# Last output projection of a two-block model as a 2x2 block product with seven multiplications

## What is computed

```python
def second_block(x, norm_g, w_in, q_norm_g, k_norm_g, rel_bias, w_out):
    ...
        mixed = jnp.concatenate([merge_heads(ya) * jax.nn.silu(ga),
                                 merge_heads(yb) * jax.nn.silu(gb)], axis=-1)
        x = x + jnp.einsum('bse,ed->bsd', mixed, w_out[layer])
    return x
```

## Time and profile before

| | |
|---|---|
| median of 3 runs | 1912.47 us (1911.5 to 1912.92) |
| profiled execution, first to last instruction (span) | 1910.9 us |
| TensorE (PE) busy | 1903.4 us, 100% of the span |
| TensorE weight loads (PEld) | 1586.7 us, 83% |
| VectorE (DVE) busy | 1172.9 us, 61% |
| ScalarE (ACT) busy | 817.9 us, 43% |
| GpSimd (POOL) busy | 112.1 us, 6% |
| last projection, first matmul to last | 1733.4 to 1907.7 us |

### The profile page before, as it was taken

The page is one execution under the profiler, slowest core; times in us unless marked ns, Lnnn a source line. Parts: engine busy times, 40 slices in busy tenths (PEclk is TensorE's granted clock), DMA queues, the critical chain, the costliest instruction groups (busy, mean ns, idle before and its releaser), DMA issues.

```text
span 1910.9 us, 27480 instructions
## 1 busy us (share of the span) xinstructions
PE 1903.4 (100%) x9126; PEld 1586.7 (83%) x9126; DVE 1172.9 (61%) x2193; ACT 817.9 (43%) x1603; POOL 112.1 (6%) x172
## 2 busy tenths in 40 slices
PE   9999999999999999999999999999999999999999
PEld 7788888888888888888888888888888888888887
DVE  6565687778877775634556565656564646466333
ACT  5653444544445434423444343434343434344211
POOL 0100011001111010001000000000000000000010
PEclk9999999999999999999999999999999999999999
DMA  8722232223232223344332222222222222223341
GB/s 323 297 89 88 78 99 78 71 71 99 77 77 77 69 73 112 123 152 143 121 116 72 91 90 88 93 88 93 88 89 92 71 102 79 88 88 121 137 160 66
DMA packets 33817, 202.09 MB, mean 106 GB/s; under 512 B 4592, under 2 KB 4720, under 8 KB 13296
## 3 DMA queue, kind: packets, MB, share of 16 engines
q1 hardware_dynamic: 23904, 165.95, 24.2%
q0 software_dynamic: 9728, 35.49, 6.8%
q10 hardware_dynamic: 144, 0.10, 0.0%
HBM read 193.10 MB, written 8.42 MB: 105 GB/s over the span
## 4 chain that ended last, share of the span: by engine, by line
PE 95%; DVE 2%; DMA 1%; ACT 1%; issue 0%; SPq 0%; DVEq 0%; ACTq 0%
PE gemm L1480 82%; PE pb L1480 12%; PE pb L1483 2%; DMA raw<-in_w 1%; DVE w_lo L829 1%; DVE act_lo L838 0%; DMA scratch<-in_memT 0%; ACT w_hi L398 0%; DVE scratch L1039 0%; ACT act_lo L435 0%; DVE parts L849 0%; DVE scratch L937 0%; ACT scratch L406 0%; ACT scratch L407 0%; ACT scratch L405 0%
## 5 line engine op out<-in xcount | busy, mean ns | idle before, releaser
L1480 PE MATMUL gemm<-act_hi,w_hi 128*128 128x512 f32 x2304 | 921.0, 400 | 0.2 <-DVE act_lo L838 0.2
L1480 PE MATMUL gemm<-act_lo,w_hi 128*128 128x512 f32 x2320 | 902.8, 389 | 0.1
L1480 PE MATMUL gemm<-act_hi,w_lo 128*128 128x512 f32 x2304 | 899.8, 391 | 0.0
L398 ACT ACTIVATE w_hi<-raw 128x512 fp32r<-128x512 f32 x616 | 337.3, 619 | 406.7 <-PE gemm L1480 385.9
L1480 PEld LDWEIGHTS gemm<-act_hi,w_lo 128*128 128x128 f32 x2304 | 432.4, 188 | 93.3
L1480 PEld LDWEIGHTS gemm<-act_lo,w_hi 128*128 128x128 f32 x2320 | 436.7, 188 | 83.4 <-ACT w_hi L398 0.4
L1480 PEld LDWEIGHTS gemm<-act_hi,w_hi 128*128 128x128 f32 x2304 | 433.4, 188 | 82.2 <-issue 0.8
L829 DVE TENSOR_TENSOR w_lo<-raw,w_hi 128x512 fp32r<-128x512 f32 x624 | 400.1, 696 | 144.7 <-ACT w_hi L398 137.2
L1480 PEld LDWEIGHTS pb<-scratch 128*128 128x128 f32 x932 | 136.0, 192 | 26.3 <-DVE scratch L1200 5.9
L1480 PE MATMUL pb<-scratch 128*128 128x128 f32 (+3 forms) x932 | 141.4, 279 | 2.2 <-DVE scratch L844 1.7
L1348 DVE SCALAR_TENSOR_TENSOR scratch<-gemm,scratch 128x512 f32<-128x512 f32 x24 | 16.6, 692 | 150.1 <-PE gemm L1480 149.9
(11 more groups left out here) (296 smaller groups left out, 1614.8 us busy)
## 6 DMA issues: line engine op xcount, KB each, us to landing
raw<-in_w SPq DMA_DIRECT2D x154, 1024.0 KB, 4.8
scratch<-in_rows_in POOLq DMA_DIRECT2D x6, 1024.0 KB, 8.5
big<-in_xT POOLq DMA_DIRECT2D x4, 1024.0 KB, 11.4
scratch<-rows POOLq DMA_DIRECT2D x16, 256.0 KB, 6.5
scratch<-in_xT POOLq DMA_DIRECT2D x16, 256.0 KB, 2.9
x<-big POOLq DMA_DIRECT2D x16, 256.0 KB, 2.3
scratch<-x POOLq DMA_DIRECT2D x16, 256.0 KB, 4.0
outT<-scratch POOLq DMA_DIRECT2D x15, 256.0 KB, 3.8
```

What stands on the lines that cost most here:

```text
L398: A(w_hi[slot][:, c], raw[slot][:, c], ACT.Copy).then_inc(sem["hi"], 1)
L1480: return nc.tensor.matmul(out, a, b, start=start, stop=stop, skip_group_check=skip)
```

## The change

The 16 output tiles are made in 8 pairs (outputs 2g and 2g+1). Of the 16 k-tiles, twelve (0 to 5 and 8 to 13) are taken as a 2x2 block product: six k-tiles against six, two outputs, and the 512 tokens in two halves of 256. The block product is made with seven products (Strassen in Winograd's form) instead of eight, each of 6 k-tiles x 3 matmuls of 256 columns. The four k-tiles 6, 14, 7, 15 (`REST`) are multiplied in the usual way, 512 columns wide, once for each output (R1, R2). The order on PE in each pair is M1 M6 M5 M7 M2 M3 R1 M4 R2 (nine products, 150 matmuls: 126 of 256 columns and 24 of 512; before 96 of 512).

New work for this: on GpSimd four sums of weight blocks per pair (each 128x768), and once the sums of token blocks, 24 operations of 128x256, during heads 6 and 7; their split into parts (`t_split`, `t_low`: six of 128x768 on each of ScalarE and VectorE); per pair on VectorE four half-width and one full-width addition that combine the products, on ScalarE one copy of M1. Weight parts are made by product, 768 columns at a time (512 for R1 and R2), in five slots instead of two buffers. SyncE loads six pieces per pair (four of 384 KB, two of 256 KB) in place of two of 1 MB. The x1 load of a pair is issued by GpSimd after that pair's four sums.

The core of the diff:

```diff
+SLOT_OF = [0, 1, 2, 3, 4, 0, 1, 2, 3]
+M1P, M6P, M5P, M7P, M2P, M3P, R1P, M4P, R2P = range(9)
+NP = 9
+T_ORDER = [0, 3, 4, 1, 2, 5]
...
+        SOURCE = [raw_t[:, A11], raw_t[:, A11], Z, raw_t[:, A21], raw_t[:, A12], Z, raw_t[:, R1W], raw_t[:, A22], raw_t[:, R2W]]
... SyncE
+            for g in range(1, PAIRS):
+                sp.wait_ge(sem["p_sum"], 4 * g)
+                for n, j in ((0, M6P), (2, M7P), (1, M2P), (4, R1P), (3, M4P), (5, R2P)):
+                    sp.wait_ge(sem["lo"], NP * g + (j + 1 - NP + HI0))
+                    pair_load(g, n)
... GpSimd
+            def w_sum(g, n):
+                if n == SUM1:
+                    pool.wait_ge(sem["piece_in2"], piece_at(2, g))
+                    pool.wait_ge(sem["piece_in3"], piece_at(3, g))
...
+                    ins = nc.gpsimd.tensor_tensor(Z, raw_t[:, A21], raw_t[:, A22], ALU.add)
+                elif n == SUM3:
...
+                    ins = nc.gpsimd.tensor_tensor(raw_t[:, A21], raw_t[:, A11], raw_t[:, A21], ALU.subtract)
+                elif n == SUM2:
+                    pool.wait_ge(sem["lo"], NP * g + (M1P + 1 + HI0))
...
+                    ins = nc.gpsimd.tensor_tensor(raw_t[:, A11], Z, raw_t[:, A11], ALU.subtract)
+                else:
+                    pool.wait_ge(sem["piece_in1"], piece_at(1, g))
+                    pool.wait_ge(sem["lo"], NP * g + (M5P + 1 + HI0))
+                    pool.wait_ge(sem["p_sum"], 4 * g + 3)
+                    ins = nc.gpsimd.tensor_tensor(Z, raw_t[:, A12], raw_t[:, A11], ALU.subtract)
+                ins.then_inc(sem["p_sum"], 1)
...
+            for kp in range(SK):
+                t_first(kp)
+            pool.wait_ge(sem["t_sum"], SK)
+            pool.wait_ge(sem["mixed"], M1 + 2 * last + 1)
+            for n in range(3):
+                t_rest(n)
+            w_sum(0, SUM1)
+            w_sum(0, SUM3)
+            pool.wait_ge(sem["b_sc"], NB * DN)
+            pool.wait_ge(sem["b_add"], NB * DN)
+            t_rest(3)
+            t_rest(4)
+            w_sum(0, SUM2)
+            pool.wait_ge(sem["b_tp"], NB * DN)
+            t_rest(5)
+            w_sum(0, SUM4)
...
+            with pool.Fori(1, PAIRS) as g:
+                w_sum(g, SUM1)
+                w_sum(g, SUM3)
+                w_sum(g, SUM2)
+                w_sum(g, SUM4)
                 for s in range(2):
+                    pool.wait_ge(sem["o2_xf"], 2 * g + (s - 1))
+                    pool.dma_start(blk(XIN2, NB * s, NB), x1_dram[2 * g + s]).then_inc(sem[f"o2_x{s}"], 16)
+                for s in range(2):
+                    pool.wait_ge(sem["evac"], 2 * g + (U_O2 - 1 + s))
+                    pool.dma_start(outT[2 * g + (s - 2)], blk(OUTS, NB * s, NB)).then_inc(sem[f"o2_st{s}"], 16)
... ScalarE
+            def pair_hi(g, j):
+                if j in (M1P, M2P, M4P, R1P, R2P):
...
+                else:
+                    act.wait_ge(sem["p_sum"], 4 * g + ({M5P: SUM1, M6P: SUM2, M7P: SUM3, M3P: SUM4}[j] + 1))
+                if j >= 5:
+                    act.wait_ge(sem["unit"], NP * g + (j - 4 + U_O2))
+                elif not isinstance(g, int):
+                    act.wait_ge(sem["unit"], NP * g + ((j + 6 if j < 4 else 5) - NP + U_O2))
...
+                A(w_slot(w_hi_all, j), SOURCE[j], ACT.Copy).then_inc(sem["hi"], 1)
+            def pair_tail(g):
+                act.wait_ge(sem["unit"], NP * g + (M1P + 1 + U_O2))
+                A(M1S, bank[0][:, 0:HALF], ACT.Copy).then_inc(sem["c_s"], 1)
+                for j in range(5, NP):
+                    pair_hi(g, j)
... VectorE, head 7
                 if last:
+                    for n in range(3):
+                        t_low(n)
+                    pair_lo(0, M1P)
                     for k in range(4):
                         operand_lo(k, 4 * KT)
...
+                    pair_lo(0, M6P)
+                    for n in range(3, SK):
+                        t_low(n)
+                    for j in (M5P, M7P, M2P):
+                        pair_lo(0, j)
+                        operand_lo(j + 10, 4 * KT)
... VectorE, projection
+            def out_base(g, s):
+                if not isinstance(g, int) or g:
+                    dve.wait_ge(sem["evac"], 2 * g + (U_O2 - 1 + s))
+                dve.wait_ge(sem[f"o2_x{s}"], 16 * g + 16)
+                V.scalar_tensor_tensor(X2[s], blk(XIN2, NB * s, NB), par[:, bass.ds(2 * g + (s + C_FIN), 1)], R1, ALU.mult, ALU.mult)\
                     .then_inc(sem["o2_xf"], 1)
+            def out_done(g, s):
+                dve.wait_ge(sem["unit"], NP * g + ((R2P if s else R1P) + 1 + U_O2))
+                dve.wait_ge(sem["c_mid"], 5 * g + (5 if s else 4))
+                V.tensor_tensor(blk(OUTS, NB * s, NB), bank[s][:, :], X2[s], ALU.add).then_inc(sem["evac"], 1)
+            def pair_middle(g):
+                pair_lo(g, 5)
...  unit M6P, then
+                V.tensor_tensor(U2, M1S, bank[1][:, 0:HALF], ALU.add).then_inc(sem["c_mid"], 1)
+                pair_lo(g, 6)
...  unit M5P, then
+                V.tensor_tensor(YX[:, HALF:S], U2, bank[0][:, HALF:S], ALU.add).then_inc(sem["c_mid"], 1)
+                pair_lo(g, 7)
...
+                pair_lo(g, 8)
...
+            def pair_next(g, first=False):
+                pair_lo(g, 0)
+                for s in range(2):
...
+                    out_done(g - 1, s)
+                    pair_lo(g, 1 + 2 * s)
+                    pair_lo(g, 2 + 2 * s)
+                    out_base(g, s)
+                pair_middle(g)
... PE
-            projection(U_O2, 4 * KT, KT // 2, False)
+                    pe.wait_ge(sem["evac"], 2 * g + (U_O2 - 1))
+                product(g, M1P, c11, True, low(lambda t: t + 1))
...
+                    pe.wait_ge(sem["evac"], 2 * g + U_O2)
+                product(g, M6P, c21, True, sums)
+                pe.wait_ge(sem["c_s"], 1 + g)
+                product(g, M5P, c12)
+                pe.wait_ge(sem["c_mid"], 5 * g + 1)
+                product(g, M7P, c22)
+                pe.wait_ge(sem["c_mid"], 5 * g + 2)
+                product(g, M2P, c11, False, low(lambda t: KT // 2 + t + 1))
+                product(g, M3P, c12)
+                product(g, R1P, a[:, :], False, low(lambda t: REST[t] + 1))
+                pe.wait_ge(sem["c_mid"], 5 * g + 3)
+                product(g, M4P, c21)
+                product(g, R2P, b[:, :])
```

More of the change, by code:

```diff
@@ L47 @@
 LEVELS = 7
+SK = 6
+HALF = S // 2
+PAIRS = KT // 2
+REST = [6, 14, 7, 15]
+WB_COLS = SK * P
+SLOT_OF = [0, 1, 2, 3, 4, 0, 1, 2, 3]
+A11, A21, R1W, A22, A12, R2W = (slice(o, o + n) for o, n in (
+    (0, WB_COLS), (WB_COLS, WB_COLS), (2 * WB_COLS, len(REST) * P),
+    (KT * P, WB_COLS), (KT * P + WB_COLS, WB_COLS), (KT * P + 2 * WB_COLS, len(REST) * P)))
+PIECES = [A11, A12, A21, A22, R1W, R2W]
+M1P, M6P, M5P, M7P, M2P, M3P, R1P, M4P, R2P = range(9)
+NP = 9
+HI0 = 4 * U_O2
+SUM1, SUM3, SUM2, SUM4 = range(4)
+T_ORDER = [0, 3, 4, 1, 2, 5]
 EARLY = (len(CONSTS) - LEVELS) * P
@@ L782, in d2_head @@
                     A(pc, pc, ACT.Exp, bias=small[:, c:c + 1], accum_out=small[:, 4 + c:5 + c]).then_inc(sem["b_exp"], 1)
-                next_hi(6)
+                if last:
+                    for n in range(3):
+                        t_split(n)
+                    pair_hi(0, M1P)
+                else:
+                    next_hi(6)
                 act.wait_ge(sem["b_vps"], h + 1)
@@ L794, in d2_head @@
                     act.wait_ge(sem["mixed"], M1 + 2 * DN - 1)
-                    for k in range(4, 12):
+                    for k in range(4, 8):
                         if k % 4 == 0:
@@ L812, in _ @@
             operand_hi(KT - 1)
-            with act.Fori(0, KT // 2 - 1) as i:
-                for j in range(2):
-                    u0 = U_O2 + j
-                    hi(2 * i + u0 + 2, u0 % 2)
+            pair_tail(0)
+            with act.Fori(1, PAIRS) as g:
+                for j in range(5):
+                    pair_hi(g, j)
+                pair_tail(g)
         @block.vector
@@ L1406, in d2_head @@
                 V.tensor_tensor(VBT, bank[slot(6)][:, :], R12, ALU.mult).then_inc(sem["evac"], 1)
-                next_lo(6)
+                if not last:
+                    next_lo(6)
                 for c in range(NB):
@@ new lines, in pair_next @@
+            def pair_next(g, first=False):
+                pair_lo(g, 0)
+                for s in range(2):
+                    if not first:
+                        dve.wait_ge(sem[f"o2_st{s}"], 16 * g - 16)
+                    out_done(g - 1, s)
[3 more added lines that the diff above has]
+                pair_middle(g)
+            for s in range(2):
+                out_base(0, s)
+            pair_middle(0)
@@ L1477, in _ @@
+            pair_next(1, True)
+            with dve.Fori(2, PAIRS) as g:
+                pair_next(g)
+            for s in range(2):
+                dve.wait_ge(sem[f"o2_st{s}"], 16 * (PAIRS - 1))
+                out_done(PAIRS - 1, s)
         @block.tensor
```

(15 more changed lines are left out.)

233 lines of the change are left out of this document (158 added, 75 removed).

## The result

The changed kernel takes 1992.97 us (median of 4 runs, 1989.92 to 1994.22) against 1912.31 for the kernel before in the same call (4 runs, 1911.50 to 1912.92): 4.2% slower, ratio 1.0418, 95% interval 1.0403 to 1.0433. The profiled execution has a span of 1988.4 us, 77.5 more than before.

What follows compares the result with a forecast made beforehand. TensorE bounded the kernel before; the change makes a ring of waits bind instead. M6 of pair 1 at 1777.4, six periods of 29.2, 20.1 for the last pair, 3.4 tail and 1.6 to the median give 1977.7 us, range 1948 to 2000.

Steps and rivals of the forecast that it cites:

- the long ring with the clock's fall: Pairs of the last projection: waits from M6 to M6 plus half-pace clock, 29.2 us a period; main forecast, 63%.
- TensorE's own work: Matmuls of a pair: 0.118 us per 256 columns, 20.3 us instead of 21.75, saving 11.6 over eight pairs.
- Side work: Per 768 columns: ScalarE copy 0.83 us, VectorE subtraction 0.96, GpSimd sum 2.0 (1.8 to 2.25).
- The ring: M6 to next M6 through parts, A22 load, sums, x1, `out_base`, `out_done`: 27.3 us, PE standing still 7.0.
- The clock: TensorE's clock falls in each pair's standstill, slowing M6 and M5: 1.9 us a pair (0 to 3.8).
- The entry: Head 7 through pair 0: PE 3 us late (0 to 5), M6 of pair 1 starting at 1777.4.
- The sum: Whole kernel: 1777.4, six periods of 29.2, last pair 20.1, tail 3.4, then 1.6 to the median: 1977.7 us.
- without the clock's loss: Rival over the pairs: same long chain of waits, no fall of TensorE's clock; 1966 us, 10%.
- all prices high: Upper end of the range: sum 2.25, load 4.5, x1 4.4 us; period 30.5 plus 3.8, reaching 2010.
- The shorter ring of 25.7: Rival: SUM2 early, only M4's end through SUM4, x1 and bank 1 binds; 1952 or 1965 us, 12%.
- Weight loads (0.188): Rival: weight loads bind the narrow matmuls at 0.188 us instead of 0.118; about 2000 us, 4%.
- TensorE as the bound: Rival: PE never waits in the pairs; 1901 to 1911 us, 6%, or 1911 to 1920 with entry stalls, 5%.

Runs made afterwards that it cites:

- experiment 1: Changed kernel with each pair's x1 loads issued on GpSimd ahead of its four weight sums, from pair 1 on; 1941.69 us, ratio 1.0155 to the kernel before.
- experiment 3: Changed kernel plus 28 unused 512-column matmuls between M1 and the wait before M6 in pairs 1 to 7; 1979.68 us.
- experiment 2: Changed kernel with VectorE's order altered so that bank 1's `out_done` stands ahead of bank 0's `out_base`; 1973.32 us.
- experiment 7: Changed kernel with x1 before the sums, earlier `out_done`, M4 before M3, entry reordered, base terms behind YX; 1921.16 us, 1.0040 to the kernel before.
- experiment 8: Changed kernel with pair 0 an ordinary product, x1 before the sums, earlier `out_done`, M4 before M3, base terms behind YX; 1916.32 us, 1.0018 to the kernel before.

## Why the prediction was right, and where it missed

1977.7 us was forecast, 1993.0 measured, within the range of 1948 to 2000. The mechanism was the one named, the long ring with the clock's fall: TensorE idle once a pair before M6, released by `out_done`, VectorE idle before `out_base` for x1. Experiments 1 and 3 bear out its two main links, x1 behind SUM4 and the clock. The number came 15.3 us too low because several terms were too small, of which the entry is the largest. Point by point:

- **TensorE's own work.** 0.118 us forecast for 256 columns, 0.120 measured (18 in 2.16). A pair is 20.58, not 20.3. The possible saving was 9.4 us, not 11.6.
- **Side work.** ScalarE 0.84 (0.83 forecast), VectorE 0.96 (0.96), a sum 1.84 (2.0 taken, 1.8 to 2.25 as bounds). By the Trainium skill, "GPSIMD Engine Reference", section "Performance versus the Vector engine", the estimate was 1.8; the rows agree with it, better than with my 2.0. (My own working for the lower bound, three times 0.6, leaves out the start-up of 0.14 and should read 1.94; what was measured lies under it.)
- **The ring**, from M6's start, forecast with the clock's loss against measured in pair 4: low part of M4 done 8.3 and 9.1, SUM1 starts 11.4 and 12.5, SUM2 ends 18.4 and 19.0, parts of M6 and M5 done 21.2 and 21.9, SUM4 ends 23.3 and 23.9, x1 there 27.5 and 29.0, M6 29.2 and 30.6. Three terms were too small: the clock, A22's load (3.1 with its issue, 3.4 measured) and x1's way, which I had at 4.3 with its issue and which took 5.15. The sums gave 0.5 back. One word on the side work was wrong: behind `out_base` stand not only low parts that TensorE wants later, but also U2, and once bank 1 no longer stood behind it (experiment 2) U2 held M7 up by 4.2 us a pair.
- **The clock.** Forecast 1.9 a pair, measured 2.6 in the period shown and 2.3 on average. That it falls in a standstill of 7 us was right. The lower level lasted 5.0 to 6.1 us behind M6's start in pairs 1 to 5 and 2.8 and 2.9 in pairs 6 and 7; I had read 3.9 from the start of the span. That the average came so near is partly luck: nothing in the prediction foresaw the two short stretches.
- **The entry** is the step that failed most. M6 of pair 1 was forecast for 1777.4 and began at 1785.6. I had costed the token differences at nothing until head 7, and they stop TensorE in head 6 already (2.9); PTL was late by 4.2, not 3; M6 of pair 0 began at 1747.5, not 1742, 2.7 of it a wait for its low part; and M7 began at 1760.7, not 1754.7, behind a standstill of 6.6. SUM4 ended at 1753.0 there, not 1747.3 (it and the low part beside it took 2.16 and 2.58 us on the port), and x1, U2 and M7 follow behind it. The clock's fall in the entry, some 6 us in all, I had costed only in part.
- **The sum.** Of the 15.3 us missed, 8.2 are there at M6 of pair 1, 4.4 are six periods that last 29.9 on average instead of 29.2, and 3.0 are the median of the runs, 4.6 above the profiled span where I put 1.6 (the profiled execution was the fastest of the four); the last stretch was 0.3 shorter. Small slips in the prediction's own sums: without the clock's loss it comes to 1964.4 and not 1966 (seven times 1.9); all prices high make the period 30.7 and not 30.5, and its upper end some 2015 and not 2010; M7 of pair 0 adds up to 1755.0 and not 1754.7; and 1586.7 us over 9126 loads is 174 ns, 188 being the mean of the loads' rows. None of them moves the range.
- **Rivals.** The shorter ring of 25.7 needed weight pieces that land at once; they took 4.2, and SUM1 waited 11.45 us for A22. Weight loads (0.188) did not bind the narrow matmuls: 0.120. TensorE as the bound, which had 11% together, did not occur either, but experiments 7 and 8 show that for every pair but the first only the order of the side work stood against it.

## What to carry to other kernels

When an edit shortens the work of the engine that binds, add up the ring of load, sum, split and next load between two of its blocks, and look at what each link stands behind on its in-order engine; here an x1 load behind four sums it had nothing to do with made 51 of an 80 us loss. Work moved to a spare engine is paid for in two more places: on the engine that shares its port, and where it must be ready for the first time, for which an ordinary first stage is a cheap cover.
